# First mixer of a three-layer kernel: one plan of weight slots, small loads on another queue

## The reference

```python
mod = cond @ ada_w[layer] + ada_b[layer]            # cond = silu(c); 1024 x 6144
shift1, scale1, gate1, shift2, scale2, gate2 = jnp.split(mod, 6, axis=-1)
h = _rms(x, norm1_w) * (1 + scale1) + shift1
qa, ka, va, qb, kb, vb, rb, ab = jnp.split(h @ w_in, ...)     # 1024 x 2320
oa = softmax over a window of 128, with rel_bias[bucket(distance)] added to the scores and a sink
log_a = log_sigmoid(ab @ gate_up + gate_bias) / 16
ob = _rms(_gla(qb, kb, vb, log_a), out_norm) * silu(rb)        # gated linear attention, chunks of 64
x = x + gate1 * (concatenate([oa, ob]) @ w_out)                # 1024 x 1024
h = _rms(x, norm2_w) * (1 + scale2) + shift2
x = x + gate2 * moe(h)      # router picks 2 of 32 experts a token; silu(h @ w1) * (h @ w3) @ w2
```

## Time and profile before

| | |
|---|---|
| median of 3 runs | 2135.22 us (2133.57 to 2136.65) |
| profiled execution | 2133.7 us, span 2131.9 us |
| TensorE busy | 1936.0 us, 91% |
| VectorE busy | 563.0 us, 26% |
| ScalarE busy | 361.5 us, 17% |
| moved | 732.34 MB, mean 344 GB/s |
| mean granted TensorE clock | 0.981 |

### The profile page before, as it was taken

How to read it: one execution, slowest core, us unless ns; L and a number is a source line. 1 busy time by engine, 2 the same in 40 slices (tenths; PEclk the granted TensorE clock), 3 DMA queues, 4 the chain that set the end, 5 groups by cost and what they waited for, 6 DMA issues and landing times. The chain is left out here.

```text
span 2131.9 us, 28620 instructions
## 1 busy us (share of the span) xinstructions
PE 1936.0 (91%) x11309; PEld 992.5 (47%) x11309; DVE 563.0 (26%) x1278; ACT 361.5 (17%) x803; POOL 2.2 (0%) x7
## 2 busy tenths in 40 slices
PE   5896999999988799999999888799999999989986
PEld 1342555544444344555544444354555555544443
DVE  2143622221112323622211122333463311111112
ACT  1141310000000123311000000214322211111111
POOL 0000000000000000000000000000000000000000
PEclk9998999999999899999999999999999999999998
DMA  9846899999999784899999999742327899999995
GB/s 321 309 158 237 358 410 426 425 427 426 426 428 424 277 295 162 353 378 424 425 428 424 427 427 425 234 146 79 119 79 280 363 424 427 425 426 427 425 428 238
DMA packets 130143, 732.34 MB, mean 344 GB/s; under 512 B 18713, under 2 KB 26748, under 8 KB 80790
## 3 DMA queue, kind: packets, MB, share of 16 engines
q1 hardware_dynamic: 130046, 731.29, 84.4%
q10 hardware_dynamic: 24, 0.02, 0.0%
HBM read 730.20 MB, written 4.23 MB: 344 GB/s over the span
## 5 line engine op out<-in xcount | busy, mean ns | idle before, releaser
L276 PE MATMUL psum<-arena,norm_w 128*64 128x256 f32 x6144 | 700.5, 380 | 51.3 <-DMA arena<-in_moe_w_dram 31.4
L276 PEld LDWEIGHTS psum<-arena,norm_w 128*64 128x64 f32 x6144 | 432.1, 136 | 318.3 <-issue 54.9
L307 PE MATMUL psum<-arena,hT 128*64 128x512 f32 x1536 | 349.7, 596 | 33.4 <-DMA arena<-in_moe_w_dram 20.1
L383 DVE TENSOR_TENSOR hT<-psum,arena 64x512 f32<-64x512 f32 x128 | 88.1, 688 | 519.5 <-PE psum L307 518.6
L307 PEld LDWEIGHTS psum<-arena,hT 128*64 128x64 f32 x1536 | 106.8, 136 | 242.8 <-issue 220.2
L466 ACT ACTIVATE hT<-psum 128x256 f32<-128x256 f32 x96 | 36.8, 383 | 1001.6 <-PE psum L276 1001.6
L327 PE MATMUL psum<-hT 128*128 128x512 f32 x384 | 177.6, 605 | 7.7 <-DVE hT L383 6.0
L2189 PE MATMUL psum<-arena,hT 128*128 128x512 f32 (+1 forms) x352 | 153.8, 587 | 2.1 <-PEq L55 1.8
L327 PEld LDWEIGHTS psum<-hT 128*128 128x128 f32 x384 | 69.0, 189 | 97.9 <-issue 85.0
L693 DVE COPY hT<-psum 128x256 f32<-128x256 f32 x96 | 40.8, 425 | 261.9 <-PE psum L295 261.9
L2189 PEld LDWEIGHTS psum<-arena,hT 128*128 128x128 f32 x352 | 65.3, 192 | 70.3 <-issue 68.3
(11 more groups left out here) (399 smaller groups left out, 1234.8 us busy)
## 6 DMA issues: line engine op xcount, KB each, us to landing
arena<-in_moe_w_dram SPq DMA_DIRECT2D x192, 2048.0 KB, 36.6
arena<-in_w_gate_dram SPq DMA_DIRECT2D x32, 2048.0 KB, 33.5
arena<-in_w_up_dram SPq DMA_DIRECT2D x32, 2048.0 KB, 34.8
arena<-in_w_down_dram SPq DMA_DIRECT2D x32, 2048.0 KB, 34.4
arena<-in_ada_w_dram SPq DMA_DIRECT2D x24, 2048.0 KB
arena<-in_w_in_dram SPq DMA_DIRECT2D x10, 2048.0 KB, 7.7
arena<-in_odd_w_in_dram SPq DMA_DIRECT2D x6, 2048.0 KB, 10.2
arena<-in_even_w_in_dram SPq DMA_DIRECT2D x4, 2048.0 KB, 14.9
```

What stands on the lines that cost most here:

```text
L276: m = nc.tensor.matmul(out[64 * half:64 * half + 64, :], xw[:, u, c, :], w[:, c, half * HALF:(half + 1) * HALF], start=(c == 0), stop=(c = ...
L307: m = nc.tensor.matmul(bank_Y[64 * half:64 * half + 64, :], hTs[:, k % 2, (k // 2) * 64:(k // 2) * 64 + 64], experts.slots[slot][2][:, k, ...
L383: return nc.vector.tensor_tensor(y[BLOCK * u:BLOCK * (u + 1), half, :], bank_Y[rows, :], gate2[rows, half * 512:half * 512 + 512], ALU.mult)
```

## The change

Four things change.

1. *Small loads.* The relative bias, the two `hot` tables, ones, ident and quads move from SyncE's to ScalarE's queue. So do the nine constants, and six of the seven small inputs that the mixer fetched for itself: they now land in the start stage, and the mixer's waits for them (`small_landed`) are gone. The bias rows are loaded in one transfer of four in the start stage and in pairs in the mixer.
2. *Bias table.* No copies inside HBM. ScalarE stores each of the two tables 32 times from SBUF (`COPIES`), and the load is four transfers of 32 partitions. The pairing of heads is done once, on the 33 x 8 input, by a copy on VectorE.
3. *One plan of slots.* `BLOCKS_0` gives each P, M and O block one of five slots. M0 and M1 are asked for in the start stage. In the mixer each wait and load is written out; a block is asked for when TensorE has used up the one that was in its slot.
4. *Expert weights.* w1 of expert 1 stands in SyncE's list behind M9, w1 of expert 0 behind M11. O0 and O1 come last, behind the uses of M9 and M10.

The orders of TensorE, VectorE and ScalarE in the mixer stay as they were.

The core of the diff:

```diff
 start_stage, SyncE
-            sp.dma_start(rb[0:REL_BUCKETS, :], rel_bias).then_inc(early_landed, 16)
...
-            for dst, src in early + [(quads, quads_dram)]:
-                sp.dma_start(dst, src).then_inc(early_landed, 16)
-            m.load(sp, slots, 0, ORDER[0] * MB, landed[0])
+            sp.dma_start(rows, m.b[:, 0:len(ORDER) * MB].rearrange("o (n w) -> o n w", w=MB)).then_inc(rows_landed, 16)
+            load_block(0)
             sp.dma_start(x, x_dram).then_inc(x_landed, 16)
             norm_w.fetch(sp, first_norm)
             for n in range(1, len(ORDER)):
-                m.load(sp, slots, n, ORDER[n] * MB, landed[n])
-            in_columns.fetch(sp)
-            for dst, src in late:
-                sp.dma_start(dst, src).then_inc(late_landed, 16)
-            skewed.spread(sp)
+                load_block(n)
+            for item in first_items:
+                blocks.load(sp, item)
+            skewed.wait_kept(sp)
             sp.wait_ge(late_landed, 16 * len(late))
 start_stage, VectorE
+            nc.vector.tensor_copy(paired.rearrange("p (a j i) -> p a i j", a=2, j=2), rb.rearrange("p (a i j) -> p a i j", a=2, i=2)
+                                  ).then_inc(heads_paired, 1)
 start_stage, ScalarE
+            act.dma_start(rb[0:REL_BUCKETS, :], rel_bias).then_inc(early_landed, 16)
...
             act.wait_ge(c_landed, 16)
             nc.scalar.activation(ccol, ccol, ACT.Silu).then_inc(c_ready, 1)
+            for dst, src in late:
+                act.dma_start(dst, src).then_inc(late_landed, 16)
 SkewedBias.store
+        for i in range(2):
+            eng.dma_start(self.scratch[i], table[:, i].unsqueeze(1).to_broadcast([HEADS, self.COPIES, SKEW])).then_inc(self.kept, 16)
 new
+BLOCKS_0 = ((("P", 0), 1), (("P", 1), 2), (("P", 2), 0), (("M", 0), 4), (("M", 1), 3), (("P", 3), 1), (("M", 2), 4), (("P", 4), 2),
+            (("M", 3), 3), (("M", 4), 0), (("M", 5), 4), (("M", 6), 1), (("M", 7), 3), (("M", 8), 2), (("M", 9), 0), (("M", 10), 1),
+            (("M", 11), 2), (("O", 0), 0), (("O", 1), 1))
 first_mixer_stage, SyncE
+            wait_made(sp, "P", 3, 1)
+            blocks.load(sp, ("M", 6))
...
+            wait_made(sp, "P", 4, 1)
+            blocks.load(sp, ("M", 8))
+            wait_made(sp, "M", 4)
+            blocks.load(sp, ("M", 9))
+            wait_kept(sp, "M", 5)
+            load_rows(4)
+            experts.load_w1(sp, 1, 1, 0)
+            wait_made(sp, "M", 6)
+            blocks.load(sp, ("M", 10))
+            wait_made(sp, "M", 8)
+            blocks.load(sp, ("M", 11))
+            wait_kept(sp, "M", 7)
+            load_rows(5)
+            experts.load_w1(sp, 0, 0, 0)
+            wait_made(sp, "M", 9)
+            blocks.load(sp, ("O", 0))
+            wait_made(sp, "M", 10)
+            blocks.load(sp, ("O", 1))
...
             experts.load_router(sp)
-            for u in range(2):
-                experts.load_w1(sp, u, u, 0)
```

More of the change, by code:

```diff
@@ L1036, with __init__ @@
 class SkewedBias:
[L1042 to L1046, removed]
+    COPIES = 32
+    def __init__(self, stage, scratch):
+        self.scratch = scratch
+        self.kept, self.landed = stage.sem("skew_kept"), [stage.sem(f"bias_landed{i}") for i in range(2)]
@@ L2068, in wait, with __init__, tile, load @@
         pe.wait_ge(self.landed[n % self.SLOTS], 16 * (n // self.SLOTS + 1))
+class Blocks:
+    def __init__(self, nc, tag, slots, order, sources):
+        self.stage, self.slots, self.sources = Stage(nc, tag), slots, sources
+        self.landed = [self.stage.sem(f"block{u}") for u in range(len(slots))]
+        self.slot, self.nth = {}, {}
+        for item, u in order:
+            self.nth[item] = 1 + sum(v == u for v in self.slot.values())
+            self.slot[item] = u
+    def tile(self, item):
+        width = self.sources[item].shape[2]
+        return self.slots[self.slot[item]][:, 0:DC * width].rearrange("p (c n) -> p c n", c=DC)
+    def load(self, sp, item):
+        sp.dma_start(self.tile(item), self.sources[item]).then_inc(self.landed[self.slot[item]], 16)
+    def wait(self, pe, item):
+        pe.wait_ge(self.landed[self.slot[item]], 16 * self.nth[item])
 def second_mixer_stage(nc, ring, x, h, hT, w, norm_w, consts, arena, psum, banks, plan, next_norm):
@@ L2858, in modulate @@
             def modulate(k):
[L2860 removed]
+                blocks.wait(pe, ("M", k))
                 bank_free("M", k)
@@ L3806, in program @@
     w_in = ins["even_w_in"][0]
-    loads = [w_in[:, a:z] for a, z in IN_0] + [ins["even_w_out"][0][:, i * 512:(i + 1) * 512] for i in range(2)]
-    ring = Ring(nc, "l0_mix", loads, arena, mark, first=1)
+    mods = [(modulations[0], j) for j in (4, 5, 8, 9, 6, 7, 10, 11)] + [(modulations[1], j) for j in range(later)]
+    columns = lambda ap: ap.rearrange("(c p) n -> p c n", p=P)
+    sources = {("P", n): columns(w_in[:, a:z]) for n, (a, z) in enumerate(IN_0)}
+    sources |= {("O", i): columns(ins["even_w_out"][0][:, i * 512:(i + 1) * 512]) for i in range(2)}
@@ new lines, in program @@
+    small = dict(quads=arena.take([P]), sinks=arena.take([HEADS]), q_norm=arena.take([64]), k_norm=arena.take([64]), out_norm=arena.take([GLA_V]),
+                 up=arena.take([GLA_HEADS * GLA_K], parts=GLA_RANK), bias=arena.take([GLA_HEADS * GLA_K], parts=1))
+    kept_from = arena.at
+    spread = [(small[t], ins[n][0].partition_broadcast(P)) for t, n in (("sinks", "a_sinks"), ("q_norm", "a_q_norm"), ("k_norm", "a_k_norm"),
+                                                                         ("out_norm", "b_out_norm"))]
@@ new lines, in program @@
+    spread += [(small["up"], ins["b_gate_up"][0]), (small["bias"], ins["b_gate_bias"])]
+    start_stage(nc, ins["c"][0], ccol, modulations[0], x, h, hT, rows(ins["x"][0]), [load(n) for n in first] + [(small["quads"], const_dram["quads"])],
+                spread + [load(n) for n in consts if n not in first], (const_dram["hot_window"], const_dram["hot_causal"]),
+                ins["rel_bias"], skewed, norm_w, ins["norm1_w"][0], blocks, [("P", 0), ("P", 1), ("P", 2), ("M", 0), ("M", 1)], arena, 0, banks, consts,
+                small["quads"])
```

167 lines of the change are left out of this document (83 added, 84 removed).

## The result

The changed kernel takes 2122.58 us (median of 5 runs, 2121.61 to 2126.97), against 2135.22 us before: ratio 0.9944, 95% interval [0.9932, 0.9956], 12.6 us faster. 2111.6 was forecast, a gain of 23.6. The profiled execution is the one of 2122.58 us, with a span of 2120.8 us. One of the six runs of experiment e6, at 2150.08 us with a granted clock of 0.933 against 0.976 to 0.982 in the others, is left out of its median.

What follows compares the result with a forecast made beforehand. Bound: TensorE between the first mixer's gaps, late block transfers in them; the expert layers by transfer rate. 0.7 + 10.5 + 7.1 + 6.5 + 6.4 - 7.6 = 23.6 us gained, 2111.6 us on the median; range 2099 to 2124.

Steps and rivals of the forecast that it cites:

- M0's gap: First mixer: the 9.28 us gap ahead of block M0 and its slow matmuls go, gain 10.5 us.
- M9: First mixer: M9 asked for at about 147 us; gap and slow group gone, less 1.7 for VectorE, gain 6.5 us.
- M11: First mixer: M11 asked for at 165.5 us, landing at 174.2, about when TensorE wants it; gain 6.4 us.
- O0 and the slow projection: Last projection of the first mixer: 5.2 us wait for O0 plus 2.4 at a lower clock, cost 7.6 us.
- Worth 0: Expert weights asked for early: two of nine blocks move forward, no gain; without cover each block is 4.9 us.
- Rival (a): No new wait: O0 is in time and SyncE does not hold the start stage; 2103 us, chance 0.22.
- rival (b): The mixer's tail queues up, each late block costing the lone 8.7 us; 14.7 us gained, 2120.5 us, chance 0.19.
- 4.0: Start stage: the new table store, 0.79 MB at the old copies' 197 GB/s, takes 4.0 us.
- about 2 us of engine time: Start stage: the late small loads add about 2 us to the sum for SyncE's end.
- - 2.1: Start stage: with small loads on ScalarE's queue the first block is issued some 2.1 us sooner.
- Cost 0: Start stage: ScalarE's 23 issues at 0.42 us end at about 14 us, before its first partial copy at 18.70.
- rival (c): Slower: ScalarE's queue backs up, at 3.96 us an issue 2160 us; decides from 2.5 us an issue; chance 0.04.

Runs made afterwards that it cites:

- e6: Changed kernel with the second mixer's bias load and norm weight asked for behind the modulation blocks they stood ahead of; 2119.43 us, ratio to before 0.9923.
- e5: Changed kernel with the two early expert blocks moved back behind O1; 2113.44 us, ratio to before 0.9895.
- e2: Changed kernel with the table store moved from ahead of ScalarE's partial copies to the end of the start stage; 2115.64 us, ratio to before 0.9906.
- e8: Changed kernel with the edits of e1 and e2 together; 2128.37 us, ratio to before 0.9963.
- e7: e4's plan of slots on the changed kernel, with the last pair of bias rows asked for ahead of O1; 2110.74 us, ratio to before 0.9876.
- e1: Changed kernel with its 6 early and 15 late small loads back on SyncE's queue; 2122.4 us, ratio to before 0.9935.
- e4: Changed kernel with O0 asked for behind M8, O1 ahead of the last bias rows, expert blocks as in e5; 2116.83 us, ratio to before 0.9914.

## Why the prediction was right, and where it was short

The mixer by itself, with times taken from its own first matmul (51.59 before, 57.32 after), each term as the prediction put it:

| term | forecast | measured |
|---|---|---|
| M0's gap | 10.5 | 10.3 |
| M6 | 7.1 | 7.2 |
| M9 | 6.5 | 8.3 |
| M11 | 6.4 | 4.8 |
| O0 and the slow projection | -7.6 | -8.0 |
| sum, to the projection's end | 22.9 | 22.6 |

(Worked from the rows: up to the end of M6's group 171.96 - 51.59 = 120.37 before, 160.20 - 57.32 = 102.88 after, and so on.)

*M0 and M6* were right; M6 was asked for at 126.46 us, near the 120 of the forecast and a mixer that starts 6.4 us behind it. *M9*: the forecast took off 1.7 us for a wait of W8 on VectorE; TensorE shows no such wait. *M11*: it still waits 1.77 us for its block, which is about the difference from 6.4. *O0*: the wait is 6.63 us and the projection 1.46 us longer, 8.1 against 7.6 forecast. The chain was right: M11 lands by 181.7, one expert block and O0 behind it take 4.9 + 5.4 = 10.3 us, and O0 is there at 192. e5 takes the one block out of it and the wait shrinks by 4.9. That "Worth 0" of the early expert weights was right as a gain, and its price of one block was in the sum, but the price was the choice most worth undoing. Rival (a) was ruled out by the 6.63 us, rival (b) by a projection that starts 10.6 us behind M11's group and not 17.4 (twice 8.7).

*The start stage* is the step that failed: a gain of 0.7 us was forecast, with a bound of 3.3 us of loss, and it lost 5.73. The structure was right (SyncE's issue ends the stage, until 56.04; the sum said 48.2, 7.8 us sooner), the sizes were not, at three terms:
- "4.0" for the store, at 197 GB/s of copies that had the engines to themselves. Here it stood beside a queue of weights, on the same engines. Taking it away brings SyncE's end from 56.04 to 49.33 us and the mixer's start from 57.32 to 51.08 (e2): 6.2 to 6.7 us instead of 4.0. That is within the "4.0 twice" of the bound, and 2.2 to 2.7 us of the miss.
- "about 2 us of engine time" for the late small loads. From 12 to 20 us both queues are busy, and the weights get 61% of the engines' time where they had 102% before; together the two queues use 74%. First after the change, then before:

```profile
q1 hardware_dynamic: 655, 1.86, 60.6%
q10 hardware_dynamic: 657, 0.29, 13.6%
```

```profile
q1 hardware_dynamic: 1187, 3.01, 101.6%
q10 hardware_dynamic: 24, 0.02, 0.9%
```

1.15 MB less of weights in 8 us are 3.0 us at 385 GB/s, and e8 gives the same by the second block (3.2 us). It is not the store: in e2, where none is issued yet, the two queues have 52.6% and 11.1% in this window. The Trainium skill, DMA: Bandwidth & Descriptors, "Queues, rings and completion order", says that a DMA engine takes turns between its queues one packet at a time. The trace agrees for this window: 655 packets of one queue and 657 of the other, though those of the second carry 440 bytes and the weights' 2840 on average. Beside the store alone the counts are not equal (1605 and 396 from 28 to 40 us). And turns don't explain why a quarter of the engines' time was idle; that stays open. The rule of the Trainium skill that the prediction cited against this part (DMA: Bandwidth & Descriptors, "Issuing engines are not separate DMA queues"), that a second issuer saves issue time only, told half: here the second queue also cost the first one rate.
- "- 2.1" for the earlier issue of the first block. It was issued 2.2 us sooner (1.57 against 3.80), but by 12 us SyncE's queue had moved 2.51 MB, against 2.64 before with 0.30 MB of small loads in it: 0.17 MB of weights ahead, or 0.4 us.

The last two terms together: with the store out of the way (e2) SyncE is done at 49.33, where the sum without the store says 44.2. By 28 us its queue has moved 6.91 MB in e2, against 8.77 less 0.30 before. That is 1.56 MB or 4.1 us behind, out of these 5.1; the last 1.0 us has no name.

*"Cost 0" for ScalarE's issues* stands, for another reason than given. They took 0.3 to 1.64 us each, three of the fifteen over 1 us, and the two stores 4.67 together, so the first partial copy came 2.2 us late. The next block was later still. The condition for rival (c), 2.5 us an issue on average, was not met: the slowest load took 1.64 us.

*The second mixer's bias load*, "0", cost 2.1 us. The forecast charged three more issues; SyncE's time up to the row is in fact the same, but the load moves at 209 GB/s where it moved at 352, ahead of a 2 KB row that the next matmul group waits for. e6 puts the load behind that row and removes the wait. Why the four pieces, read from 32 copies instead of 128, move more slowly no run separates.

*Behind the first refill* the prediction assumed that all shifts are kept. From 266.76 to the output 2125.95 it is 1859.2 us before, and 1863.6 after. Of these 4.4 us the second mixer's wait is 2.1. The rest is no term of the change that I can name: in the ten experiments this stretch took between 1855.1 (e6, whose second mixer doesn't wait) and 1866.3 us (e7), with nearly the same instructions. The third mixer's first projection is 3.0 us slower at the lower clock, but of these only 0.7 are left at the output (shifts of -11.82 and -11.09). What decides on which matmuls such a low stretch falls was not settled.

Together: 23.6 forecast; 22.6 won in the mixer, 5.7 lost before it, 1.3 right behind it (a group of the router's matmuls, L269, at 5.71 us instead of 4.35), 2.1 in the second mixer, 2.3 in the rest: 11.1 between the profiled spans, 12.6 between the medians. Of the marks set beforehand for a wrong step, the first mixer matmul after 55 us came about as written; of the issues on ScalarE three of fifteen loads took over 1 us, not each; a gap ahead of O1 did not come.

That 2122.6 lies inside the range of 2099 to 2124 owes something to luck. The upper end was made of rival (b), which did not happen, and a loss of 3.3 us in the start stage. The measured time came about by a larger loss there and by losses behind the first refill, which the sum had at nothing.

## What to carry to other kernels

When small transfers or a store move to a second queue, charge them to the first queue at more than their bytes: 0.59 MB of the store took 1.40 MB from the stream of large blocks beside it, and 0.29 MB, mostly of small loads, took 1.15 MB. Put a store that nobody reads until the next stage behind the last load that the stage is waiting for (e2), and see that no small loads are left to be issued beside it (e8). And in a list of loads, what lies one place ahead of the block that ends the wait costs its whole transfer: a 2 MB block for a later loop there cost 4.9 us, a row of 4 KB placed behind 4 MB cost 5.1.

## What the runs showed of the hardware

- From 12 to 20 us, with small loads on the second queue, the engines were busy for 74% (64% in e2), against 102% with one queue, at nearly equal packet counts (655 and 657; 525 and 527 in e2). From 20 to 28 us the same two queues together stood at 108%.
- The store's packets of 1536 bytes held 31% of the engines' time for 15% of the bytes from 28 to 40 us (0.59 MB beside 3.24), so the engines were full at 319 GB/s in place of 387. With little beside it (e8, 48 to 62 us) the store moved 0.77 MB in 14 us and took 43% of the engines' time.
- The first issue on SyncE's queue behind the blocks P0 to P2 took 4.24 us (e8) and 5.29 us (e1) for a load of 4 KB. Beside the late store a load of 16 KB took 4.11 us to issue (e8). On ScalarE's queue each of the same loads took 0.3 to 1.64 us.
- A 4 KB row behind two 2 MB blocks landed 11.6 us after its issue (e4).
- The slanted load moved at 209 GB/s in four pieces of 32 partitions from 32 copies, and at 352 GB/s in one piece from 128 copies, with the engines full both times.
